# A two-block transformer kernel on one core: TensorE's side steps moved from the middle of a weight unit to its end

## The reference

```python
h = rms_norm(x, norm_g)
proj = h @ w_in                      # split into 13 pieces
y_a = mla_branch(c_q, c_kv, k_rope, ...) * silu(z_a)      # attention, 8 heads
y_b = sgu_branch(gelu(u_b), gelu(v_b), v_g, w_s, b_s) * silu(z_b)
y_c = gla_branch(q_c, k_c, v_c, a_r, ...) * silu(z_c)     # gated linear attention, 4 heads
merged = g[0] * (y_a @ w_branch[0]) + g[1] * (y_b @ w_branch[1]) + g[2] * (y_c @ w_branch[2])
x = x + merged @ w_out
```

## Time and profile before

| | us |
|---|---|
| median of three runs | 3650.35 |
| lowest, highest run | 3643.81, 3651.71 |
| the profiled execution's own time | 3643.81 |
| its span in the profile | 3641.7 |
| PE busy | 3476.0 |
| DVE, ACT, POOL busy | 2383.4, 1648.9, 880.5 |
| mean granted PE clock | 0.971 |

### The profile page before, as it was taken

The page is one execution under the profiler, slowest core; times in us unless marked ns, Lnnn a source line. Parts: engine busy times, 40 slices in busy tenths (PEclk is TensorE's granted clock), DMA queues, the critical chain, the costliest instruction groups (busy, mean ns, idle before and its releaser), DMA issues.

```text
span 3641.7 us, 67295 instructions
## 1 busy us (share of the span) xinstructions
PE 3476.0 (95%) x28672; PEld 3457.5 (95%) x28672; DVE 2383.4 (65%) x3061; ACT 1648.9 (45%) x2035; POOL 880.5 (24%) x904
## 2 busy tenths in 40 slices
PE   7999999889999899879899999999999999999999
PEld 7999999789999899779899999999998999999999
DVE  7766754668878744774777755555647877655554
ACT  4334434443368734444445444444435444444443
POOL 4741211124346511220432310000103323100000
PEclk9999999899999999889899999999999999999999
DMA  5555555345545555445344455555553444555554
GB/s 187 181 183 185 182 200 193 132 162 174 181 167 185 183 196 186 133 130 171 129 158 140 142 180 185 186 185 191 168 183 130 138 141 149 169 185 191 186 186 168
DMA packets 167482, 619.28 MB, mean 170 GB/s; under 512 B 18576, under 2 KB 18704, under 8 KB 166544
## 3 DMA queue, kind: packets, MB, share of 16 engines
q1 hardware_dynamic: 164880, 600.13, 49.2%
q10 hardware_dynamic: 2304, 14.85, 1.1%
HBM read 610.71 MB, written 4.19 MB: 169 GB/s over the span
## 4 chain that ended last, share of the span: by engine, by line
PE 52%; DVE 2%; issue 1%; POOL 1%; ACT 1%; DMA 0%; POOLq 0%; ACTq 0%; DVEq 0%
PE banks L470 16%; PE banks L462 16%; PE banks L463 16%; PE pm L522 1%; DVE xs L1077 0%; PE pm L611 0%; DVE wide L1087 0%; PE pm L643 0%; PE pm L644 0%; PE pm L642 0%; PE ms_bank L483 0%; PE pm L495 0%; DVE w_lo L1053 0%; PE pm L594 0%; PE pm L626 0%
## 5 line engine op out<-in xcount | busy, mean ns | idle before, releaser
L1053 DVE TENSOR_TENSOR w_lo<-raw,w_hi 128x1024 fp32r<-128x1024 f32 x1144 | 1509.2, 1322 | 956.3 <-ACT w_hi L758 922.8
L758 ACT ACTIVATE w_hi<-raw 128x1024 fp32r<-128x1024 f32 x1144 | 1204.3, 1057 | 1126.4 <-PE banks L470 1097.8
L462 PE MATMUL banks<-xs,w_hi 128*128 128x256 f32 x5728 | 1433.4, 287 | 102.9 <-DVE xs L1077 97.6
L463 PE MATMUL banks<-xs,w_hi 128*128 128x256 f32 x5728 | 1426.8, 286 | 0.0
L462 PEld LDWEIGHTS banks<-xs,w_hi 128*128 128x128 f32 x5728 | 1115.0, 195 | 111.6 <-issue 73.2
L463 PEld LDWEIGHTS banks<-xs,w_hi 128*128 128x128 f32 x5728 | 1116.5, 195 | 0.2
L470 PE MATMUL banks<-xs,w_lo 128*128 128x256 f32 x5728 | 828.7, 287 | 0.0
L470 PEld LDWEIGHTS banks<-xs,w_lo 128*128 128x128 f32 x5728 | 752.3, 195 | 0.5
L462 PE MATMUL banks<-inner,w_hi 128*128 128x256 f32 x1408 | 340.3, 281 | 20.6 <-ACT w_hi L758 16.7
L463 PE MATMUL banks<-inner,w_hi 128*128 128x256 f32 x1408 | 339.4, 281 | 0.0
L462 PEld LDWEIGHTS banks<-inner,w_hi 128*128 128x128 f32 x1408 | 269.5, 191 | 21.2 <-ACT w_hi L758 17.1
(11 more groups left out here) (281 smaller groups left out, 4152.4 us busy)
## 6 DMA issues: line engine op xcount, KB each, us to landing
raw<-weights SPq DMA_DIRECT2D x1144, 512.0 KB, 3.3
wide<-x_in ACTq DMA_DIRECT2D x2, 2048.0 KB, 9.4
x_scratch<-wide ACTq DMA_DIRECT2D x1, 2048.0 KB, 8.4
wide<-x_scratch ACTq DMA_DIRECT2D x1, 2048.0 KB, 7.9
out_x<-wide ACTq DMA_DIRECT2D x1, 2048.0 KB, 6.3
w_st<-w_s ACTq DMA_DIRECT2D x2, 512.0 KB, 5.2
b_st<-b_s ACTq DMA_DIRECT2D x2, 512.0 KB, 7.1
tab<-tables ACTq DMA_DIRECT2D x1, 548.5 KB, 3.4
```

Source lines behind the costliest of these rows:

```text
L462: nc.tensor.matmul(bank, w_hi[:, slot, w], x[:, 0:T], start=(k + t == 0), stop=False)
L463: nc.tensor.matmul(bank, w_hi[:, slot, w], x[:, T:2 * T], start=False, stop=False)
L758: nc.scalar.activation(w_hi[:, slot, :], raw[:, slot, :], ACT.Copy).then_inc(hi_done, 1)
L1053: nc.vector.tensor_tensor(w_lo[:, slot, :], raw[:, slot, :], w_hi[:, slot, :].bitcast(F32), ALU.subtract).then_inc(lo_done, 1)
```

## The change

In `products`, the call that runs the side steps is taken from between the high and the low matmuls of a unit's first piece, and is put behind the last piece of the unit, behind the increment of `pe_mark`. It is called with the unit's own number, where it was called with that number less one. A step due at Y thus stood inside unit Y+1 and stands now between unit Y and unit Y+1. DVE's, ACT's and POOL's programs are untouched.

```diff
@@ -462,8 +462,6 @@
                             nc.tensor.matmul(bank, w_hi[:, slot, w], x[:, 0:T], start=(k + t == 0), stop=False)
                             nc.tensor.matmul(bank, w_hi[:, slot, w], x[:, T:2 * T], start=False, stop=False)
                         if c == 0:
-                            if side is not None:
-                                side.run(at_unit(s, i, u) - 1)
                             pe.wait_ge(lo_done, unit)
                         for t in range(n):
                             w = slice((c + t) * P, (c + t + 1) * P)
@@ -471,6 +469,8 @@
                                                    start=False, stop=(k + t == p.depth - 1))
                         ins.then_inc(pe_mark, 1)
                         k += n
+                        if side is not None and c + n == UNIT_TILES:
+                            side.run(at_unit(s, i, u))
                     if j == 0 and after_first is not None:
                         after_first()
```

## The result

The changed kernel takes 3661.48 us (median of 18 runs, 3653.3 to 3671.0); beside it the kernel before takes 3643.22 us (median of 18, 3633.43 to 3651.71). The ratio is 1.0051, with a 95% interval of 1.0041 to 1.0061: 18.3 us slower by the medians, where +22 was forecast. The profiled execution after took 3657.43 us, its span is 3655.2 us, and its mean granted clock 0.972, where before it was 0.971.

A forecast was written before the change was run, and what follows sets the result against it. PE, busy 95% of the span, was taken as the bound; 9.1 us of added waits a layer, 18.2 over two, plus 4 for the clock made 22, so 3650.35 became 3672 us (own range 3662 to 3682; 8 in 10: 3658 to 3686).

The forecast's parts named there:

- R-E: Last input's end plus 0.1 us (R) less unit Y's end (E); cost max(0, R-E-1.92) before, max(0, R-E) after.
- transposes due at 4, 5: PE comes 1.6 us too early, but unit 13's 1.77 us wait for a weight split swallows the delay: 0.
- scores 0: Score matmuls due at 12, already waiting for POOL's product of decays and keys: full cap, +1.92 us a layer.
- scores 1: Score matmuls due at 17, behind PE's own mean square: chain moves along, POOL's product slower beside DVE, +0.5 us.
- scores 3: Score matmuls due at 27, which waited 2.26 us before: full cap, +1.92 us a layer.
- scores 5: Score matmuls due at 37 in the 4-deep stages, 0.33 us wait before: cap of 8 matmuls, +0.96 us.
- bank behind q_buf: PE's 2.4 us wait for a PSUM bank ends with a DVE backlog independent of side steps: it stays.
- spatial mixes: Second pair, due at 59, waits for DVE to read the first pair from PSUM: +1.92 us a layer.
- three more stretches at half clock: New or lengthened PE waits bring three low-clock stretches over both layers: +4 us, bounds -4 (present ones go) and +17.
- clock runs away: Rival: each of twelve lengthened or new PE waits brings one further low-clock stretch, 35 us slower, 3685 us; chance 0.15.
- Absorbed: Rival: added waits let ACT and DVE catch up and shorten PE's next wait; within 0.2%, 3656 us; chance 0.09.
- faster: Rival: earlier side results let ACT and DVE reach splits sooner, PE's main-stream waits go; 3642 us; chance 0.04.

The follow-up runs named there:

- x1: Against the kernel before, only latent norms and GLA steps moved to the end of unit Y, spatial gate and attention as before: 3653.1 us, ratio 1.0031.
- x2: Against the kernel before, only spatial gate and attention moved to the end of unit Y, norms and GLA as before: 3645.3 us, ratio 1.0015.
- x5: Against the changed kernel, every PE side step one unit sooner, at the end of unit Y-1: 3847.58 us, ratio to the kernel before 1.0568.
- x3: Against the kernel before, only the latent norms (mean squares due at 17 and 19) moved to the end of unit Y: 3633.58 us, ratio 0.998.
- x9: Norms at the end of unit Y, GLA at Y+2, the rest at Y+1: 3635.18 us, ratio to the kernel before 0.9987.
- x4: Against the changed kernel, every PE side step one unit later, at the end of unit Y+1: 3626.03 us, ratio to the kernel before 0.9958.
- x6: Against the changed kernel, norms stay at the end of unit Y, everything else goes to Y+1: 3620.99 us, ratio to the kernel before 0.9954.
- x10: Against the changed kernel, only the eight score steps due one unit later (13+5n): 3630.71 us, ratio to the kernel before 0.9969.

## Why the prediction was right, and where its sizes were off

The mechanism stood: PE is in order, a step that waits now holds up high matmuls that had been done under the wait, and what it costs is R-E, at most 1.92 us a place. The forecast of +22 us was +18.3; the waits of the side stretches grew by 9.3 and 7.3 us, where 9.1 were worked out for each. Place by place (third layer; wait after less wait before, us):

| step | predicted | measured |
|---|---|---|
| transposes due at 4, 5 | 0 | +1.2 |
| scores 0 | +1.92 | 5.95 - 1.77 - 3.12 = +1.06 |
| scores 1 | +0.5 | 2.96 - 3.40 = -0.44 |
| GLA output 0 | +0.78 | +0.6 |
| scores 3 | +1.92 | 4.16 - 2.26 = +1.90 |
| scores 5 | +0.96 | 1.86 - 0.33 = +1.53 |
| bank behind q_buf | 0 | +1.0 |
| scores 7 | +1.09 | +0.90 |
| spatial mixes | +1.92 | 1.0 + 0.3 = +1.3 |
| sum | 9.1 | 9.1 |

That the two sums of this layer agree is luck: six places are off by half a us or more, and up and down cancel. In the fourth layer scores 0 cost only 0.56 us more (5.94 - 1.77 - 3.61), scores 1 nothing (-0.08) and the bank nothing.

**Transposes and scores 0** belong together: PE was late by the 1.2 us that the transposes cost, and the wait behind them grew by 1.06 us instead of 1.92. The two make +2.26, where 1.92 was forecast; most of the delay was swallowed, 0.86 us of it. The forecast gave 6.1 us for the single wait if PE came 1.6 late, and it was 5.95.

**Scores 1** had the wrong sign. I expected POOL's product to take longer for meeting DVE's work sooner. POOL's timeline after at this place, which answers to the earlier trace rows:

```profile
1762.77 2.34 POOL L1631 TENSOR_TENSOR g_d<-g_d,gqk 128x1024 f32<-128x1024 f32 x1
```

It took 2.34 us, less than the 2.78 before, and the wait shrank by that 0.44. It was DVE that paid. DVE's timeline after:

```profile
1760.34 2.35 DVE L1053 TENSOR_TENSOR w_lo<-raw,w_hi 128x1024 fp32r<-128x1024 f32 x2
...
1762.95 3.20 DVE L1144 TENSOR_TENSOR g_d<-b_cum 128x256 f32<-128x256 f32 x2
```

The same pair before:

```profile
1769.15 0.75 DVE L1144 TENSOR_TENSOR g_d<-b_cum 128x256 f32<-128x256 f32 x2
```

The pair takes 0.75 us alone and 3.20 beside POOL's product; it starts 0.18 us after the product and ends 1.04 behind it. Around scores 0 it is the other way: DVE's two-input work starts first, and the product takes 3.2. The Trainium skill (SBUF — State Buffer, Who interferes with whom) says that the two engines shut each other out for a whole instruction; these rows agree, and who starts first decides who pays. In the prediction I had read the 2.35 to 3.38 us of the earlier trace rows as evidence against that rule. They are not: 2.34 is the product that went first, 3.3 one that waited for the rest of a single DVE instruction. So the earlier trace rows could not show what DVE pays.

**Scores 5 and the bank.** In the third layer PE waited 1.0 us more for a bank just ahead. It stood nearer behind DVE from there on, so the same POOL product came 0.6 us later after the end of PE's unit than before (R-E is 2.0, and was 1.4). In the fourth layer the bank wait did not grow, and scores 5 went from 0.70 to 1.57 us, +0.87, near the cap. Here the assumption that E and R move together failed by half a us.

**Spatial mixes**: 1.3 of 1.92. One of the steps, due at 59, waits 1.03 us for DVE's read, and another, due at 57, 0.30 for ACT. Here too R and E did not move together: beside before, the end of unit 59 lies 1.10 us earlier (1929.48, 1930.58) and DVE's read 1.88 us (1930.14, 1932.02). Most likely DVE's work starts from an earlier mark of PE, and PE lost time behind it, some of it at 57.

**The clock.** I took +4 us for three more stretches at half clock. In these two executions the time at half clock in the side stretches is the same before and after, 30.7 us in the third layer and 34.1 in the fourth: some places gained one, others lost one, as the bound of "some drop" allowed. The granted clock on record for every run says the same: 0.9723 and 0.9717 in the mean of x1's and x2's runs, and 0.9718 for the kernel before beside them, where 0.001 is 7 us at half clock; the change's own 18 runs have 0.9712, and one run of the kernel before beside them has 0.971. So a term of a few us can't be excluded, and none is seen. The 1.9 and 1.4 us by which PE's busy time grew are not in that number. The rule by R-E leaves them out; a part is the first matmul behind a wait, which takes 0.39 us and not 0.28, at six more waits in the third layer. The rest I did not follow. So of the +4 some 1.7 (18.3 less 16.6 of waits) to 3.3 us were there, and they have another name than the clock. The rival "clock runs away" was wrong here: every one of the waits above, and no more low clock. In x5, with 71 us more of waits in each side stretch, the time at half clock rose from 65 to 188 us: there it did run away. The Trainium skill (TensorE: Matmul & The Clock Gate, HAM oscillation) has this behaviour for idle gaps between bursts, and x5 agrees; at the size of the change's waits no more of it showed than before.

"Absorbed" and "faster" fell: of the seven places only the pair above was absorbed in part, and scores 1 turned for its own reason; ACT's waits for side results shrank (3.1 us for the attention sums in the third layer, 6.9 before) without PE gaining. What the "faster" rival got right is that an earlier result can pay. x3 shows where: at the mean square, since POOL's product stands behind it in the chain.

## What to carry to other kernels

In an engine that runs its program in order and is the bound, a side step costs what its last input is late (and, in these runs, what the clock adds or gives back), and moving its call by a fraction of a unit changes that at every place at once. Work out for each step how late the last input comes after the unit's end, and give each kind of step its own moment: late for consumers with a long chain ahead (the scores), early for those that release such a chain (the mean square). Moving GLA one unit later still no longer paid: in x9 the waits moved to the main stream, most likely because ACT, which feeds it, now waits for the late results.

## What was not expected of the hardware

A lead of a fifth of a microsecond was enough to decide which of two engines pays when both read SBUF. DVE's split started 0.22 us ahead of POOL's product at scores 0 (1738.30, 1738.52), and POOL paid; DVE's pair started 0.18 us behind it at scores 1, and DVE paid. In the rows read here, POOL's 128x1024 product takes 2.34 us where it went first, and 3.2 to 3.4 where a two-input DVE instruction did; DVE's pair takes 0.75 us or 3.20.

In the kernels that got faster, low clock was a large share of the gain. In the kernel before, the third layer's stretches at half clock lie in units 13 (10.2 us), 18 (6.8), 28 (6.8) and 34 (3.4), each behind or at one of PE's waits, and in 62 (3.4), behind the one-column matmuls of the attention sums. In the fourth layer such a stretch stands behind each of the four blocks of those matmuls, without any wait; the prediction speaks of one.

PE's busy time in the 24 side stretches of the twelve kernels is 387 us plus 0.56 us for each us that PE was busy at half clock (a fit, residuals of 0.9 us in the mean and 2.0 at most; 0.49 without x5). By this fit a stretch of 3.41 us costs 1.7 to 1.9 us, where the prediction took 1.4. In the profiled executions the time at half clock in both stretches together went from 65 us before to 41 in x4 and x6 and 38 in x10. PE's busy time fell by 11.9, 13.0 and 7.0 us, out of 14.4, 21.0 and 10.9 us by which the two stretches became shorter.

The profiled execution of the kernel before had a rather low clock, 0.971. Over all runs the mean is 0.9718, 0.9725 and 0.9728 in the three groups, and 0.9742, 0.9741 and 0.9752 for x4, x6 and x10 beside them. That makes 18, 13 and 18 us less at half clock in a whole execution. At 0.56 it is an estimated 10, 7 and 10 us, of the 15, 17 and 11 gained. Shorter waits go with it, but not in proportion (x9 waits longer than before and has 44 us in its side stretches). Which gap brings a low stretch and which does not stays open.
